# Modulation rows as VectorE dot products in the projection, the bonus ahead of the scaled keys, and query products in halves behind every group of gathered rows

## The chip, the cores and the metric

The kernel runs on one core of a Trainium2 chip, as one launch. The time is the device time of that core in microseconds, taken as the median of three runs. All data are 32-bit; "PE" is TensorE, "DVE" VectorE, "ACT" ScalarE, "POOL" GpSimd and "SP" SyncE, which here only issues DMAs. Line numbers (L...) are those of the kernel before.

## The reference, cut to what matters

One layer over 512 latent tokens and 256 context tokens of width 1024:

```
m = silu(c) @ w_mod + b_mod                       # 6 x 1024: shift, scale, gate, shift2, scale2, gate2
hx = rms_norm(x) * (1 + sc1) + sh1                # rows 1 and 2 (context: from c_ctx)
zx = hx @ w_in                                    # the projection, 3 x 1024 + lora columns + gates
k_dir = k * (1 + (iclr - 1) * k_a)                # per direction
bonus = sum(r * mean(k_dir) * r_k) * v            # per head of 64
... RWKV-7 scan in both directions, box pooling, sigmoid gates, output projection ...
x = x + gt1 * rms_norm(mix)                       # rows 3 of the modulation
hx2 = rms_norm(x) * (1 + sc2) + sh2               # rows 4 and 5
q = hx2 @ w_q; s = q . sub_keys                   # 8 heads x 2 halves, 128 keys each
top 16 of each half, top 16 of the 256 sums -> 16 experts per head and token
act = gelu(u_emb[idx] . hx2); out = sum(gate * act * v_emb[idx])
x = x + gt2 * rms_norm(out)                       # row 6
```

The last four of the six modulation rows (gt1, sh2, sc2, gt2; 4096 numbers, for `c` alone) are what the first part of the change computes in another way and at another place.

## The kernel before, in words

The stages follow each other with a barrier between: `front` (norm and the first two modulation rows), `project` (72 to 378 us), `gates` (to 530), `invert` (to 788), `scan`, `mix` (to 1292) and `peer` (to the end).

**`project`** works through 27 weight tiles (128 columns by 1024), 3 for the lora inputs and 3 for each of 8 head pairs j. Per tile SP loads the raw weights, ACT makes the high part (`high`, L446), DVE the low part (`low`, L553), PE multiplies 24 times per segment (`product`, lines 91 to 93), ACT copies with a scale (`scaled`, L451), DVE adds the shifted tokens (`shift`, L560 and L563). The order on every engine is written out by hand. DVE's iteration j does, for the tiles of pair j and for the vectors of pair j-1: shift, low, `unit`, `keys` (with the operand `tb` of the bonus), `queries`; `summed`, shift, low, `bounded`, `keys_out` (L620), `bonus` (L626); shift, low, `removal` (L635), `addition` (L642, L647). Three waits tie the others to it: ACT's first `scaled` of pair j waits for `addition` of pair j-2, its third `scaled` of pair j waits for `bonus(j-1)`, and PE's second `lora` of pair j waits for `bonus(j-1)`. The factor `kf` of the keys has two buffers. Results go to DRAM per field and pair, by SP, which waits for each in the order of its list.

**`invert`** inverts 32x32 blocks on DVE, in two halves b of 31 steps (L1136, L1138: a product and a sum per step); PE and ACT turn tiles before and after. Beside that PE makes the eight half rows of 512 of the last four modulation rows (`row`, L1226: one output partition, 8 products of 512 columns each), from 16 loads of 1 MB by SP; ACT copies each (L1094), PE turns it into a column (`column`, L1232), and DVE adds bias and gains (`columns`, L1120 to L1123). Two rows are made before the first half is turned out, six after it. `columns` stands in DVE's program between two steps of the second half:

```
if b and u == HB - 10:
    columns()        # first instruction: dve.wait_ge(s_col, NR)
```

**`peer`** has 32 steps s = 8 t + h (token tile t, head h), each of four groups q of four gathered rows (a gather brings 128 rows of 8 KB, u and v of one expert, 1.05 MB, issued by POOL at L2114 into a ring of 12 slots, of 16 from the second token tile on; a slot is free when PE has used it). Per group: four DVE dots (L2276), ACT gelu (L2186), DVE `gc_` (L2282), ACT four diagonal matrices (L2191), PE 8 products into the output (L2383, here V group). Queries and scores of all tokens are made in the first eight steps: three heads ahead of step 0, then in step s the head s+3: PE does `query(s+3, 0)` before V group 2, `query(s+3, 1)` before V group 3 (24 products each), and `score(s+3)` (L2362) behind V group 3. ACT, behind its work for group 3, copies query and scores (L2161, L2169 to L2175) and makes `exp(s+2)`, which needs two loads of its function table (L2037, L2186), and only then comes the gelu of the next step's group 0. DVE makes `best`, `pairs` and `numbers` of step s+2 behind groups 0, 1 and 2. In a step with queries SP also loads 2 x 0.52 MB of query weights and stores 0.39 MB of scores.

Of the kernel before, what the change touches and what calls it, by code (L numbers as in the profile page):

```python
# [95 lines left out]
def build(nc, x, ctx_in, gvec_in, wmod, wlora_in, wpair_in, pvec_in, lora_in, wz_in, wpool_in,  # L96
# [15 lines left out]
    with top:  # L112
# [15 lines left out]
        sc = sb(top, "sc", [P, KT, 2])  # L128
# [25 lines left out]
def front(nc, sb, sem, g):  # L154

    gv, mod, sc, ident, blk, bank, ht_hi, ht_lo = (g[k] for k in (
        "gv", "mod", "sc", "ident", "blk", "bank", "ht_hi", "ht_lo"))
    NB = 4
    with ExitStack() as st:
# [4 lines left out]
        modrow = sb(st, "modrow", [2, NB * 512])  # L164
        th = sb(st, "th", [P, 16])
# [131 lines left out]
def project(nc, sb, sem, g):  # L297
    gv, blk, bank, ht_hi, ht_lo, record = (g[k] for k in ("gv", "blk", "bank", "ht_hi", "ht_lo", "record"))
# [4 lines left out]
    with ExitStack() as st:  # L303
# [12 lines left out]
        kf = sb(st, "kf", [P, 2, NDIR, T])  # L316
# [8 lines left out]
        rec = sb(st, "rec", [P, RC_N])  # L325
        chunks = lambda a: a.rearrange("p (c s) -> p c s", s=CHUNK)
# [39 lines left out]
        with nc.Block() as block:  # L366
            @block.sync
            def _(sp):
# [18 lines left out]

                weights(0)
                weights(1)
                weights(2)  # L390
                sp.dma_start(pva[:, :, :], g["pvec_in"].rearrange("j p v -> p j v")).then_inc(s_pv, 16)
                lora_weights(0)
                lora_weights(1)
                for n in range(3, 8):
                    weights(n)
                for j in range(NPAIR + 1):
                    if j + 1 < NPAIR:
                        weights(3 * j + 8)
                    if j:
                        sp.wait_ge(s_r, 2 * j)  # L400
                        stored("r", j - 1)
                    if j < NPAIR:
                        sp.wait_ge(s_gc, j + 1)
                        stored("g", j)
                    if j + 2 < NPAIR:
                        weights(3 * j + 9)
                    if j:
# [5 lines left out]
                    if j + 2 < NPAIR:  # L413
                        weights(3 * j + 10)
                    if j:
# [9 lines left out]
                    if j + 2 < NPAIR:  # L425
                        lora_weights(j + 2)
                for f in FIELDS:
# [11 lines left out]
            def _(act):  # L439
# [50 lines left out]
                def rates(j):  # L490
# [5 lines left out]
                    for d in range(NDIR):  # L496
                        act.wait_ge(s_at, 4 * j + 2 * d + 2)
                        act.activation(kf[:, j % 2, d, :], al[:, j % 2, d, :], ACT.Identity, bias=col(j, OKA),
# [8 lines left out]
                high(1)  # L507
                act.wait_ge(s_vec, 1)
# [34 lines left out]
                exps(NPAIR - 1)  # L543

            @block.vector
            def _(dve):
# [46 lines left out]
                def keys(j):  # L593
                    k = zs[:, j % 2, 1, :]
                    for d in range(NDIR):
                        dve.wait_ge(s_kf, 2 * j + d + 1)
                        for C, view in parts(d):
                            o = chunks(kf[:, j % 2, d, :])[:, C, :]
# [4 lines left out]
                    ch(dve.tensor_tensor(tb[:, :], kf[:, j % 2, 0, CTX:T], kf[:, j % 2, 1, CTX:T][:, ::-1], ALU.add))  # L603
# [1849 lines left out]
```

## Time and profile before

| | |
|---|---|
| median of 3 runs (lowest, highest) | 2697.44 us (2691.69, 2699.06) |
| the profiled execution | 2706.24 us, its span 2704.5 us |
| granted TensorE clock, mean | 0.897 of full |
| busy share of the span | PE 81%, DVE 60%, ACT 32%, POOL 26% |
| moved by DMA | 741.53 MB, of it 536.90 MB by gathers |

The busy shares are means over stages with different limits, so a stage is read by itself: its busy time in a stretch (windows), the order of its instructions (timeline), and behind each instruction the time its engine sat idle and what ended that, in square brackets. PEclk 1.00 is the full clock of 2.4 GHz, 0.50 is 1.2 GHz. Start times are from the start of the span.

### The profile page before, as it was taken

To read this page: it belongs to the slowest core of one execution; us is meant where nothing else is said; L and a number is where in the kernel's file an instruction comes from. 1 tells how busy PE (TensorE), PEld (TensorE's weight loads), DVE (VectorE), ACT (ScalarE), POOL (GpSimd) and SP (SyncE) were. 2 spreads that over 40 slices of the span, in tenths; PEclk is the share of its full clock that TensorE was granted. 3 is DMA by queue.
4 is the path that set the end of the run, shared out by engine and by line. 5 is a ranking of instruction groups with operands and counts; after the bars stand their busy time and mean duration, and the time that the engine had idled before them with its cause. 6 is when DMAs were issued, how large, how long until landed. Compare 5 with 4: busy or idle time off the path is not lost.

```text
span 2704.5 us, 41392 instructions
## 1 busy us (share of the span) xinstructions
PE 2177.9 (81%) x16681; PEld 1362.7 (50%) x16681; DVE 1632.4 (60%) x3421; ACT 855.6 (32%) x1668; POOL 714.6 (26%) x607
## 2 busy tenths in 40 slices
PE   6899959887768989978789888777777777877777
PEld 2777748675258888857545443333232223333332
DVE  2489864358302434355486677777777777777764
ACT  4476733244143333422322222212212212222211
POOL 0000027000001111100233344544343444444441
PEclk8899979975858998979899999899998998888998
DMA  4245453252435242243699999999999999999995
GB/s 172 89 162 211 187 200 120 100 203 90 158 119 209 93 151 89 81 157 118 252 393 387 356 365 420 401 420 420 421 420 420 421 420 421 421 420 421 422 421 218
DMA packets 128832, 741.53 MB, mean 274 GB/s; under 512 B 17120, under 2 KB 24320, under 8 KB 60032
## 3 DMA queue, kind: packets, MB, share of 16 engines
q0 software_dynamic: 73728, 536.90, 48.2%
q1 hardware_dynamic: 53760, 199.89, 20.3%
q8 instruction: 131, 2.15, 0.3%
q10 hardware_dynamic: 1152, 2.10, 0.2%
q14 instruction: 61, 0.50, 0.1%
HBM read 683.14 MB, written 55.69 MB: 273 GB/s over the span
## 4 chain that ended last, share of the span: by engine, by line
DMA 28%; PE 15%; DVE 3%; issue 3%; ACT 2%; POOL 1%; POOLq 0%; DVEq 0%; ACTq 0%
DMA uv<-in_uv_in,ic 18%; PE bank L2383 12%; DMA uvx<-in_uv_in,ic 10%; DVE junk L2276 1%; PE bank L91 1%; PE bank L92 1%; PE bank L93 1%; POOL uv L2114 1%; DMA scores_dram<-later 1%; ACT dg L2191 0%; PE bank L2362 0%; ACT ge L2186 0%; ACT L2186 0%; DVE wql L2242 0%; POOL uvx L2114 0%
## 5 line engine op out<-in xcount | busy, mean ns | idle before, releaser
L2383 PE MATMUL bank<-uv,dg 128*128 128x512 f32 x1664 | 808.2, 642 | 230.7 <-ACT dg L2191 230.5
L2383 PEld LDWEIGHTS bank<-uv,dg 128*128 128x128 f32 x1664 | 333.4, 205 | 696.0 <-issue 395.5
L2276 DVE SCALAR_TENSOR_TENSOR junk<-uv,gr 128x1024 f32<-128x1024 f32 x416 | 509.8, 1225 | 218.1 <-DMA uv<-in_uv_in,ic 194.7
L2114 POOL DMA_INDIRECT uv<-in_uv_in,ic x416 | 462.5, 1112 | 648.7 <-PE bank L2383 583.1
L2186 ACT ACTIVATE ge<-dt_ 128x4 f32<-128x4 f32 x128 | 26.3, 205 | 928.7 <-DVE junk L2276 928.7
L2383 PE MATMUL bank<-uvx,dg 128*128 128x512 f32 x384 | 191.2, 656 | 62.6 <-ACT dg L2191 62.6
L2191 ACT ACTIVATE dg<-ident,gc_ 128x128 f32<-128x128 f32 x512 | 163.6, 390 | 29.4 <-DVE gc_ L2282 29.4
L91 PE MATMUL bank<-ht_hi,wh 128*128 128x256 f32 (+1 forms) x432 | 151.2, 350 | 22.9 <-DVE wl L553 22.9
L2383 PEld LDWEIGHTS bank<-uvx,dg 128*128 128x128 f32 x384 | 78.1, 209 | 175.6 <-issue 93.2
L2114 POOL DMA_INDIRECT uvx<-in_uv_in,ic x96 | 108.9, 1135 | 144.1 <-PE bank L2383 134.6
L92 PE MATMUL bank<-ht_lo,wh 128*128 128x256 f32 (+1 forms) x432 | 146.2, 338 | 0.0
L93 PE MATMUL bank<-ht_hi,wl 128*128 128x256 f32 (+1 forms) x432 | 145.8, 338 | 0.0
L2276 DVE SCALAR_TENSOR_TENSOR junk<-uvx,gr 128x1024 f32<-128x1024 f32 x96 | 117.5, 1224 | 41.8 <-DMA uvx<-in_uv_in,ic 37.7
L91 PEld LDWEIGHTS bank<-ht_hi,wh 128*128 128x128 f32 x432 | 82.8, 192 | 44.1 <-DVE wl L553 23.0
L818 POOL MEMSET uu<- 128x1920 f32 x4 | 6.6, 1703 | 308.1 <-POOLq L109 308.1
L92 PEld LDWEIGHTS bank<-ht_lo,wh 128*128 128x128 f32 x432 | 82.8, 192 | 9.4 <-issue 1.9
L93 PEld LDWEIGHTS bank<-ht_hi,wl 128*128 128x128 f32 x432 | 82.7, 191 | 8.7
L1368 POOL TENSOR_TENSOR lv<-lk,ec 128x1536 f32<-128x1536 f32 x8 | 22.1, 2761 | 238.4 <-PE bank L1601 238.4
L2282 DVE TENSOR_TENSOR gc_<-ge,pe_ 128x4 f32<-128x4 f32 x128 | 20.9, 163 | 97.8 <-ACT ge L2186 97.8
L91 PE MATMUL bank<-ht_hi,wzh 128*128 128x512 f32 x160 | 65.2, 408 | 17.9 <-DVE wzl L917 17.9
L1136 DVE TENSOR_TENSOR gm<-gz,gt 96x124 f32<-96x124 f32 (+15 forms) x62 | 55.2, 890 | 33.3 <-ACT gt L1060 31.1
L917 DVE TENSOR_TENSOR wzl<-wz,wzh 128x1024 fp32r<-128x1024 f32 x20 | 29.3, 1464 | 69.6 <-ACT wzh L866 69.6
(334 smaller groups left out, 3869.4 us busy)
## 6 DMA issues: line engine op xcount, KB each, us to landing
pair_record<-rec SPq DMA_DIRECT2D x40, 768.0 KB, 3.3
wm<-in_wmod SPq DMA_DIRECT2D x16, 1024.0 KB, 5.1
wraw<-in_wpair_in SPq DMA_DIRECT2D x24, 512.0 KB, 3.6
ab<-pair_record SPq DMA_DIRECT2D x16, 768.0 KB, 6.4
wz<-in_wz_in SPq DMA_DIRECT2D x20, 512.0 KB, 3.3
wm<-in_wmod SPq DMA_DIRECT2D x4, 2048.0 KB, 21.1
wraw<-in_wq_in SPq DMA_DIRECT2D x16, 512.0 KB
uv<-in_uv_in,ic POOLq DMA_INDIRECT x416, 27.6
```

The lines of the kernel that those rows point to most:

```text
L91: tensor.matmul(out, w_hi, x_hi, start=first, stop=False)
L92: tensor.matmul(out, w_hi, x_lo, start=False, stop=False)
L93: return tensor.matmul(out, w_lo, x_hi, start=False, stop=last)
L917: dve.tensor_tensor(wzl[:, n % 2, :, :], wz[:, n % 2, :, :], wzh[:, n % 2, :, :].bitcast(FP32), ALU.subtract).then_inc(s_lo, 1)
L1136: ch(dve.tensor_tensor(o, gz[:, :, 0:n, u:u + 1].broadcast_to((NU, 4, n, m)), gt[b][:, :, u:u + 1, n:HB].broadcast_to((NU, 4, n, m)), ALU. ...
L1368: pool.tensor_tensor(lv[:, :, :, :], lk[:, :, :, :], wide, ALU.mult).then_inc(s_kp, 1)
L2114: pool.indirect_dma_start(ring(i), None, g["uv_in"], bass.IndirectOffsetOnAxis(ap=ic[:, s % ICR, k:k + 1], axis=0)).then_inc(su[row_slot[i ...
L2186: act.activation(ge[:, GR * q:GR * q + GR], dt[:, GR * q:GR * q + GR], ACT.Gelu).then_inc(s_ge, 1)
L2191: act.activation(dg[:, n % 2, k, :], ident[:, :], ACT.Copy, scale=gc[:, n % 2, k:k + 1]).then_inc(s_dg, 1)
L2276: dve.scalar_tensor_tensor(junk[:, :], ring(i)[:, 0:D], 1.0, hc[:, t % 2, :], ALU.mult, ALU.mult, accum_out=dt[:, k:k + 1]).then_inc(s_ud, 1)
L2282: dve.tensor_tensor(gc[:, n % 2, :], ge[:, GR * q:GR * q + GR], rt.pe[:, s % ICR, GR * q:GR * q + GR], ALU.mult).then_inc(s_gc, 1)
L2383: mm = pe.matmul(acc(t, c)[:, :], dg[:, n % 2, k, :], ring(i)[:, D + 512 * c:D + 512 * c + 512], start=h == 0 and q == 0 and k == 0, stop= ...
```

## The change

1. The eight `row` products, their copies, `column` and `columns` leave `invert`, with their 16 loads. In `project` each of the 32 columns of 128 modulation values becomes one DVE dot product over 1024 elements, against silu(c) spread over all partitions; a transposed copy of the weights is loaded, 32 loads of 0.52 MB through three buffers. Four dots stand in each of DVE's iterations 0 to 7. `columns` stands in iteration 8 ahead of `removal`; PE turns the result and SP stores it at the stage's end.
2. In `project`, `bonus(j-1)` stands ahead of `keys_out(j-1)`, and `kf` has one buffer, for whose release ACT waits (`s_k`).
3. In `peer`, PE does half of a query product (12 products) behind every V group of steps 0 to 4, and the scores of head s+2 behind V group 0 of step s (1 to 5). ACT copies query 1 and scores and makes `exp(s+1)` behind its work for group 0, and copies query 0 behind group 2. DVE's `best`, `pairs`, `numbers` move one group later, `low` to groups 1 and 3.

```diff
@@ project, DVE @@
+                def dot(m):
+                    if m >= NM:
+                        return
+                    dve.wait_ge(s_wt[m % MR], 16 * (m // MR) + 16)
+                    if m:
+                        dve.wait_ge(s_dot, m)
+                    dve.scalar_tensor_tensor(cond[:, :], wt[:, m % MR, :], 0.5, silu[:, :], ALU.mult, ALU.mult,
+                                             accum_out=mc[:, m:m + 1]).then_inc(s_dot, 1)
...
                         low(3 * j + 5)
+                    dot(4 * j)
                     if j:
                         unit(j - 1)
                         keys(j - 1)
                         queries(j - 1)
+                    dot(4 * j + 1)
                     if j < NPAIR:
                         summed(j)
                         shift(3 * j + 4)
                         low(3 * j + 6)
                         bounded(j)
-                    if j:
+                    dot(4 * j + 2)
+                    if j:
+                        bonus(j - 1)
                         keys_out(j - 1)
-                        bonus(j - 1)
                     if j < NPAIR:
                         shift(3 * j + 5)
                         low(3 * j + 7)
+                    dot(4 * j + 3)
+                    if j == NPAIR:
+                        columns()
                     if j:
                         removal(j - 1)
                         addition(j - 1)
@@ project, SP @@
+                def row_weights(m):
+                    if m >= NM:
+                        return
+                    if m >= MR:
+                        sp.wait_ge(s_dot, m - MR + 1)
+                    sp.dma_start(wt[:, m % MR, :], g["wrow_in"][m]).then_inc(s_wt[m % MR], 16)
...
+                    row_weights(4 * j + 3)
                     if j:
                         sp.wait_ge(s_r, 2 * j)
                         stored("r", j - 1)
+                    row_weights(4 * j + 4)
@@ project, ACT, rates(j) @@
                         act.wait_ge(s_at, 4 * j + 2 * d + 2)
+                        if j:
+                            act.wait_ge(s_k, 2 * j)
@@ invert, DVE @@
-                        if b and u == HB - 10:
-                            columns()
@@ invert, PE @@
-                for n in range(EARLY):
-                    row(n)
                 turned_out(0)
                 combined(0)
-                pe.wait_ge(s_zc, 12)
-                column(0)
-                for n in range(EARLY, NR):
-                    row(n)
-                    column(n - 1)
-                column(NR - 1)
...
@@ peer, ACT @@
-                    if q >= 2 and s + 3 < HEADS:
-                        query(s + 3, q - 2)
+                    if q == 0 and 1 <= s and s + 2 < HEADS:
+                        query(s + 2, 1)
+                        score(s + 2)
+                    if q == 2 and s + 3 < HEADS:
+                        query(s + 3, 0)
...
-                if s + 3 < HEADS:
-                    score(s + 3)
-                if s + 2 < NS:
-                    exp(s + 2)
+                    if q == 0 and 1 <= s and s + 1 < NS:
+                        exp(s + 1)
@@ peer, DVE @@
-                    if q < 2 and s + 3 < HEADS:
-                        low(s + 3, q)
+                    if s == 0 and q == 0:
+                        low(3, 0)
+                    if q == 1 and s + 3 < HEADS:
+                        low(s + 3, 1)
+                    if q == 3 and s + 4 < HEADS:
+                        low(s + 4, 0)
...
-                    elif s + 2 < NS and q < 3:
-                        (best, pairs, numbers)[q](s + 2)
+                    elif s + 2 < NS and q > 0:
+                        (best, pairs, numbers)[q - 1](s + 2)
@@ peer, PE @@
                 for q in range(NQ):
-                    if q >= 2 and s + 3 < HEADS:
-                        query(s + 3, q - 2)
                     for k in range(GR):
...
-                if s + 3 < HEADS:
-                    score(s + 3)
+                    if q == 0 and 1 <= s and s + 2 < HEADS:
+                        score(s + 2)
+                    if s + 3 < HEADS:
+                        query(s + 3, q // 2, range(KT // 2 * (q % 2), KT // 2 * (q % 2) + KT // 2))
```

## Rows read from the trace of the kernel before

**Rows 1.** The profile's page, part 2: GB/s moved, in 40 slices of 67.6 us.

```profile
GB/s 172 89 162 211 187 200 120 100 203 90 158 119 209 93 151 89 81 157 118 252 393 387 356 365 420 401 420 420 421 420 420 421 420 421 421 420 421 422 421 218
```

**Rows 2.** Projection: busy us (x) of PE, PEld, DVE, ACT, POOL; PEclk, DMA share, GB/s.

```profile
172.00:327.00 155.00, 155.00 (x831) 122.76 (x829) 139.13 (x198) 111.43 (x164) 0.00 (x0) 1.00 0.53 198
```

**Rows 3.** Timeline of VectorE in the projection: start us, us, engine line op [idle before].

```profile
239.73 1.33 DVE L560 SCALAR_TENSOR_TENSOR zs<-bank,vva,zs 128x255 f32<-128x255 f32 x2 [1.02 <-ACT zs L451]
...
261.13 1.33 DVE L560 SCALAR_TENSOR_TENSOR rec<-bank,vva,rec 128x255 f32<-128x255 f32 x2 [1.83 <-ACT rec L451]
...
271.14 1.33 DVE L560 SCALAR_TENSOR_TENSOR zs<-bank,vva,zs 128x255 f32<-128x255 f32 x2 [1.02 <-ACT zs L451]
...
355.36 1.33 DVE L560 SCALAR_TENSOR_TENSOR rec<-bank,vva,rec 128x255 f32<-128x255 f32 x2 [2.97 <-ACT rec L451]
```

**Rows 4.** Timeline of VectorE in the router stage, one step.

```profile
1446.92 0.16 DVE L2282 TENSOR_TENSOR gc_<-ge,pe_ 128x4 f32<-128x4 f32 x1 [13.21 <-ACT ge L2186]
...
1453.15 0.08 DVE L2276 DVE_READ_ACCUMULATOR junk<-uv,gr 128x1 f32 x1
...
1457.52 0.16 DVE L2282 TENSOR_TENSOR gc_<-ge,pe_ 128x4 f32<-128x4 f32 x1 [0.27 <-ACT ge L2186]
...
1458.74 0.42 DVE L2012 TENSOR_TENSOR cand<-sv 128x256 f32<-128x256 f32 x1
...
1467.23 0.17 DVE L2282 TENSOR_TENSOR gc_<-ge,pe_ 128x4 f32<-128x4 f32 x1 [0.27 <-ACT ge L2186]
...
1470.95 1.22 DVE L2276 SCALAR_TENSOR_TENSOR junk<-uv,gr 128x1024 f32<-128x1024 f32 x1
...
1477.30 1.23 DVE L2276 SCALAR_TENSOR_TENSOR junk<-uv,gr 128x1024 f32<-128x1024 f32 x1
```

**Rows 5.** Timeline of VectorE in the inversion, around the column products.

```profile
683.04 1.02 DVE L1138 TENSOR_TENSOR gz<-gz,gm 96x828 f32<-96x828 f32 x1
725.65 0.77 DVE L1120 TENSOR_TENSOR colv<-bank,gv 128x8 f32<-128x8 f32 x4 [41.59 <-PE bank L1232]
...
727.17 0.95 DVE L1136 TENSOR_TENSOR gm<-gz,gt 96x768 f32<-96x768 f32 x1
```

**Rows 6.** Timeline of TensorE in the inversion, second half.

```profile
738.34 3.56 PE L1181 MATMUL bank<-ident,gz 96*128 96x96 f32 x20 [10.91 <-DVEq L1141]
```

**Rows 7.** Busy time of three stretches of the router stage, columns as in rows 2.

```profile
1345.00:1398.00 53.00, 44.77 (x128) 24.35 (x128) 41.49 (x112) 15.64 (x33) 18.37 (x16) 0.92 1.01 420
1398.00:1594.00 196.00, 172.77 (x512) 95.17 (x512) 130.19 (x312) 50.70 (x121) 69.83 (x64) 0.94 0.95 367
1594.00:1628.00 34.00, 29.81 (x59) 12.40 (x60) 30.16 (x76) 8.79 (x25) 15.97 (x14) 0.88 0.93 370
```

**Rows 8.** Timeline of TensorE in the router stage.

```profile
1441.26 1.95 PE L2362 MATMUL bank<-wor,qt_ 128*128 128x128 f32 x16
1447.57 8.83 PE L2383 MATMUL bank<-uv,dg 128*128 128x512 f32 x16 [4.36 <-ACT dg L2191]
...
1465.60 0.39 PE L93 MATMUL bank<-o_hi,wql 128*128 128x512 f32 x1
...
1470.51 0.40 PE L93 MATMUL bank<-o_hi,wql 128*128 128x512 f32 x1
...
1496.41 8.73 PE L2383 MATMUL bank<-uv,dg 128*128 128x512 f32 x16 [4.36 <-ACT dg L2191]
...
1647.66 7.13 PE L2383 MATMUL bank<-uv,dg 128*128 128x512 f32 x16 [3.00 <-ACT dg L2191]
...
1667.53 10.20 PE L2383 MATMUL bank<-uv,dg 128*128 128x512 f32 x16 [2.79 <-ACT dg L2191]
```

**Rows 9.** Timeline of ScalarE in the router stage.

```profile
1442.35 0.38 ACT L2169 ACTIVATE sc_<-bank 128x256 f32<-128x256 f32 x1 [6.22 <-PE bank L2362]
...
1443.86 1.28 ACT L2037 ACT_TABLE_LOAD   x1
...
1446.68 0.20 ACT L2186 ACTIVATE ge<-dt_ 128x4 f32<-128x4 f32 x1
```

More of the change, by code:

```diff
@@ L395, in _ @@
                     weights(n)
+                for m in range(MR):
+                    row_weights(m)
                 for j in range(NPAIR + 1):
@@ L507, in _ @@
                 high(1)
+                act.wait_ge(s_cb, 16)
+                act.activation(silu[:, :], cond[:, :], ACT.Tanh, scale=0.5).then_inc(s_cth, 1)
                 act.wait_ge(s_vec, 1)
@@ L543, in _ @@
                 exps(NPAIR - 1)
+                act.wait_ge(s_ct, 1)
+                act.activation(rw[:, :], bank[6][0:NM, 0:P], ACT.Copy).then_inc(s_rw, 1)
             @block.vector
@@ L1217, in combined @@
                         mm.then_inc(s_z, 1)
-                def row(n):
-                    for i in range(2):
-                        pe.wait_ge(s_wm[i], 16 * n + 16)
-                        if i == 0 and n >= 2:
-                            pe.wait_ge(s_rwc, n - 1)
-                        for k in range(KT // 2):
-                            c = KT // 2 * i + k
-                            mm = pe.matmul(bank[4 + n % 2][0:1, :], sc[:, c, 0:1], wm[:, i, k, :], start=c == 0, stop=c == KT - 1)
-                        mm.then_inc(s_rp, 1)
-                def column(n):
-                    pe.wait_ge(s_rwc, n + 1)
-                    for i in range(4):
-                        mm = pe.matmul(bank[6][:, 4 * n + i:4 * n + i + 1], rowv[:, n % 2, i * P:i * P + P], ident[0:1, 0:1],
-                                       start=True, stop=True)
-                    mm.then_inc(s_col, 1)
                 products(0)
@@ L2342, in _, with query @@
         def _(pe):
[L2343 to L2347 removed]
+            def query(h, b, ks=range(KT)):
+                if 0 in ks:
+                    pe.wait_ge(s_lo, 2 * h + b + 1)
+                    if h:
+                        pe.wait_ge(s_qc, 2 * h - 1 + b)
+                for k in ks:
                     mm = split_mm(pe, bank[2 + b][:, :], wh[:, b, k, :], wl[:, b, k, :], h2h[:, k, :], h2l[:, k, :],
                                   k == 0, k == KT - 1)
[L2350 removed]
+                if KT - 1 in ks:
+                    mm.then_inc(s_q, 1)
             def score(h):
```

112 lines of the change are left out of this document (44 added, 68 removed).

## The prediction

> **What bounds the kernel now.** I read the page's slices first, then busy time by stretch, then timelines. The slices show two kinds of kernel: until about 1285 us the DMA is far from its best, and from slice 21 to the last but one it moves 356 to 422 GB/s, mostly 420 [rows 1]. So the end is set by 512 gathers that stream at 420 GB/s, and an earlier stage is worth what it brings forward the start of that stream; within the stream only time counts in which the DMA is not full.
>
> The projection is bound by PE: in 155 us PE is busy for 155.00 at full clock, DVE for 139.13 [rows 2]. Its period is 271.14 - 239.73 = 31.41 us, and DVE idles in it twice, for 1.02 and 1.83 us [rows 3]. The inversion is bound by DVE, and there DVE stands still for 41.59 us: `columns` waits for the last column product while 8 steps of the second half are still to do [rows 5]. PE starts to turn that half out only when DVE is done, after 10.91 us idle [rows 6]. In the router stage step 0 runs at a full DMA (420 GB/s), steps 1 to 4 at 367 and step 5 at 370 [rows 7].
>
> **The inversion.** Without `columns` DVE goes on at 684.06 (683.04 + 1.02) instead of at 727.17 [rows 5]: 43.1 us. Late next could be PE, but its column work is gone too, and the wait in [rows 6] is for DVE alone; the store of the first half is issued when its copies end, before PE's column products began, so by DVE's order it is long past by then. The two rows made before the first half is turned out go as well; PE waited for DVE there, so nothing more is gained. I take -43.1, bounds -36 (if DMA or turning out shows up behind it) and -44.
>
> **The dots.** DVE gets 32 products of 1024 elements with a sum. The same form is in the trace: 1.23 us and 0.08 for the reading of the sum [rows 4], 1.31 each, 5.24 per period. DVE's period without its idle time is 31.41 - 2.85 = 28.56; with 5.24 of dots 33.8. That is over PE's 31.41, so DVE becomes the bound. Of the idle time I keep 0.5: DVE's first shift needs ACT's copy, which waits for `addition` just ahead of it, and the 1.02 in [rows 3] has both that copy and PE's lateness. The 1.83 goes, since `bonus` now stands ahead of `keys_out`: ACT may copy while DVE scales keys. The period is 34.3, +2.9. Pair 0 has room for its four dots (pair 1's vectors don't exist yet, DVE mostly waits); pairs 1 to 6 pay 6 x 2.9 = 17.6. In pair 7 the last two tiles have no low part and DVE idles 2.97 [rows 3], which takes most of three dots (3.9); the fourth is paid: 2.3. `columns` ahead of the last `removal` costs what it did, 727.17 - 725.65 = 1.5 [rows 5]; turning and storing its result lies beside 5.7 us of DVE work and the last stores. Sum +21.4.
>
> Moved past it: each row load on SP waits for a dot three back, which DVE has then passed; SP's list follows DVE's order, so neither stores nor weight loads fall behind. The DMA has room, at a share of 0.53 [rows 2]. ACT's new wait, with the last of its work of pair j queued behind it, is for `keys_out(j-1)`, which ends some 2 us after `bonus`; ACT first copies, makes a high part and tanh after `bonus`, so it costs nothing. If DVE gets later still, both get later together. Least: if dots overlap their neighbours and the sum is read for nothing, 1.1 each, +16. Most: PE. Its second `lora` waits for `bonus`, so that it now stands some 3 us per period (estimate from DVE's order). V groups behind idle times of 3.00 and 2.79 us took 7.13 and 10.20 us [rows 8]: the clock may stay or fall, at up to 3 us a time. PE's lead at that point is some 2 us, so at most 1 us per period shows, +29 with a little for waits. I take +21.4.
>
> **The clock.** The Trainium skill ("TensorE: Matmul & The Clock Gate", Why this matters for your kernels) says that an idle stretch between bursts puts the array back to half clock; by that rule each of seven gaps costs, and the projection would get some 28 us longer instead of 21. The trace bears it out in part: one of the two gaps above cost nothing. It is the base of two rivals.
>
> **The queries.** Four facts of a step of 48.84 us (1496.41 - 1447.57) [rows 8]: DVE stands 13.21 us before the first `gc_` [rows 4]; the scores stand behind V group 3 (1441.26) and ACT's copies and two table loads behind them (1442.35 to 1446.68 [rows 9]); PE idles 4.36 us and starts V group 0 at low clock, 8.83 us, where others take 7.13 [rows 8]. After the change I count from `gc_` of group 0. V group 0 starts at 0.65 (1447.57 - 1446.92) and ends at 7.8. PE makes the scores, ACT's copy can start 1.1 later, and from copy to gelu is 4.33 [rows 9]: 13.2, `gc_` at 13.4. Then `best` with one low part, dots, gelu: 10.6 (1457.52 - 1446.92), 24.0. Then `pairs` without a low part: 9.71 - 1.22 = 8.5, 32.5. Then low, `numbers` (3.72), gates (0.83) and dots (5.52): 11.3, 43.8 [rows 4]. PE needs four V groups of 7.13, scores of 1.95 [rows 8] and two queries of 24 products, 5.6 each (21 products start in the 4.91 us between two rows): 41.7. The DMA needs 16 x 1.05 + 1.05 + 0.39 = 18.2 MB, 43.3 us at 420. So 44 us per step, near a full DMA; 4.8 us gained, in step 4 6, since it has one low part less. In step 0 V group 2 no longer waits for a query, and step 1 starts some 6 us earlier, but the DMA is full there, so that is room, not time. Step 5 pays: it has scores but no queries, so by the same counts (no low parts) some 41 us for DVE, where the stretch before took about 34 [rows 7]. Its DMA needs 17.2 MB, 40.9 us at 420, so little shows.
>
> What counts is the DMA's empty time: 196 x (420 - 367)/420 = 24.7 us in steps 1 to 4, 34 x 50/420 = 4.0 in step 5 [rows 7], together 28.8, the most that can come. By my steps 0.7 us stays in each of three steps, 1.4 in step 4 and some tenths in step 5, about 4; I leave 6 for unevenness of a ring of 12, so -23, bounds -29 and 0. After step 8 `numbers` and gates meet behind group 3: 9.9 us of DVE against 10 of DMA per group, with 16 slots as cover; nothing.
>
> The Trainium skill ("ScalarE: Activation LUTs", What ACT_TABLE_LOAD costs) prices a change of table at about 2.66 us with a drain. By that `exp` would hold group 1 for 2.8 us longer, a step would take 46.6 and about 10 us of the gain would go. The row has 1.28, and the exponential's whole detour from 1443.86 to 1446.68 is 2.82 [rows 9]; I use the row.
>
> **Sum.** -43.1 + 21.4 - 23 = -44.7. The profiled execution took 2706.24 (span 2704.5); it would take 2661.5. That execution stands 8.8 above the median, 2697.44, which I carry over: 2652.7, say 2653. From no change, this measurement can tell about 0.3%, 8 us.
>
> **Rivals.** (A) *The query part is hidden or trades one wait for another.* The scores' wait moves from before group 0 to before group 1, 13.4 us against 10.6 for a group of that kind; if the ring of 12 empties there, only some 3 us come. 43.1 - 21.4 + 3 = 25: 2672. For it: DMA share is already 0.95 [rows 7]. Against: the rate in GB/s is not. 0.2.
> (B) *DVE in the projection costs more than its length*, by PE's clock or by ACT's `kf` wait: +29 to +32. 43 - 31 + 21 = 33: 2664. 0.14.
> (C) *Slower.* The gap ahead of the second `lora` takes PE to 1.2 GHz and keeps it there: a period, all of it PE [rows 2, 3], would take up to twice 31.41, less the part in which the gap has not yet told, some 53 us in all. 7 x 21.6 = +151, against it 43 and 23: 2782. It decides where low clock fills over half of each period, +74 in the stage. Against: after 4.36 us idle V group 0 took 8.83 and the next ran full, so PE recovers within a group [rows 8]. 0.04.
> (D) *The inversion doesn't do what it says*: the 41.59 us turn into a wait for something that the trace hides behind it; +21 - 23: about 2697. For it nothing but that the wait hides it. 0.05.
> (E) The forecast, 0.57.
>
> **Range and chances.** The forecast's own bounds: -44 + 16 - 29 = -57, and -36 + 29 - 10 = -17; with a few us of spread of the median, 2637 to 2680. That takes in A and B and leaves out C, D and the outer ends, 0.15 to 0.2. A, B and E are faster by over 0.3%: with D's better half 0.9. Same 0.05, slower 0.05.
>
> **What would show it.** Right: `columns` in the projection, no wait of 41 us in the inversion, whose second half ends 43 us sooner after its start; dots of 1.31 us; a projection period near 34.3 with DVE never idle beyond 0.5 us, PE idle some 3 us ahead of the second `lora`; steps 1 to 4 at 44 us with 410 GB/s or more, the wait before group 1 at 7 us on DVE. Wrong: a period beyond 35.5 (clock or waits), dots that wait for their rows (SP's order), steps still at 47 or more, or a new wait in the inversion on PE or a store.

## The result, and the profile after

The changed kernel takes 2652.56 us (median of 4 runs, 2647.50 to 2666.96); the kernel before took 2696.35 in the same comparison. The ratio is 0.984, interval 0.9813 to 0.9867: 36 to 50 us shorter. Forecast: 2653, 44.7 shorter. The profiled execution has a span of 2653.7 us against 2704.5.

By stage, from the start times of the same instruction in both traces (us; a step is measured from `gc_` to `gc_`):

| stage | before | after | change | forecast |
|---|---|---|---|---|
| front, to the first shift | 115.0 | 112.9 | -2.1 | 0 |
| projection, to the first instruction of gates | 266.9 | 283.1 | +16.2 | +21.4 |
| gates | 188.5 | 189.2 | +0.7 | 0 |
| inversion, first step to the scan's first DVE sum | 228.7 | 186.0 | -42.7 | -43.1 |
| scan and mix, to the first `gc_` | 545.6 | 545.3 | -0.3 | 0 |
| router, steps 0 to 7 | 364.6 | 340.2 | -24.4 | -23 |
| router, the rest | 995.2 | 997.0 | +1.8 | 0 |

**Slices.** The same line of the page as [rows 1]:

```profile
GB/s 175 146 205 251 245 200 162 83 215 1 49 180 158 111 134 137 36 177 110 267 420 417 408 393 415 415 420 420 421 420 420 421 420 420 420 420 421 421 420 209
```

Where the line of before dips to 356 and 365 in slices 23 and 24, this one dips to 408 and 393.

**Projection.** DVE in one period of the kernel after (timeline, columns as in [rows 3]):

```profile
244.11 1.33 DVE L594 SCALAR_TENSOR_TENSOR zs<-bank,vva,zs 128x255 f32<-128x255 f32 x2 [0.65 <-ACT zs L479]
...
247.54 1.22 DVE L690 SCALAR_TENSOR_TENSOR cond<-wt,silu 128x1024 f32<-128x1024 f32 x1
248.68 0.08 DVE L690 DVE_READ_ACCUMULATOR cond<-wt,silu 128x1 f32 x1
248.68 1.01 DVE L625 SCALAR_TENSOR_TENSOR uk<-zs,vva,rn 128x768 f32<-128x768 f32 x1
...
267.03 1.28 DVE L594 SCALAR_TENSOR_TENSOR rec<-bank,vva,rec 128x255 f32<-128x255 f32 x2
...
277.64 1.33 DVE L594 SCALAR_TENSOR_TENSOR zs<-bank,vva,zs 128x255 f32<-128x255 f32 x2 [0.54 <-ACT zs L479]
```

The period is 277.64 - 244.11 = 33.53, forecast 34.3. Both idle times of [rows 3] answer here: 1.02 became 0.54, 1.83 is gone. A dot costs 1.14, from 247.54 to the start of the next instruction, not 1.31: the sum's reading starts at 248.68, and so does `unit`. Four times 0.17 is 0.7 of the 0.8 us by which the period is shorter than forecast. From 176 to 345 us the only thing that DVE waits for is ACT's first copy: it never waits for a row load, nor ACT for the release of `kf`.

PE now waits ahead of the second `lora` (timeline of TensorE):

```profile
231.80 2.94 PE L770 MATMUL bank<-lin,lw 64*128 64x256 f32 x8 [2.06 <-DVE rec L660]
265.44 1.57 PE L770 MATMUL bank<-lin,lw 64*128 64x256 f32 x8 [0.55 <-DVE rec L660]
298.98 1.92 PE L770 MATMUL bank<-lin,lw 64*128 64x256 f32 x8 [2.06 <-DVE rec L660]
```

It waits 0.5 to 2.1 us, where 3 were estimated, and the eight products took 2.94 once and 1.92 once instead of 1.57: a dip of the clock. Behind the last of these rows it reaches into the next weight tile, whose first twelve products take 0.35 to 0.58 us (mostly 0.41) instead of 0.28, up to 303.5. The period from 210.47 to 244.11 has a granted clock of 0.95, the next one 1.00, and yet they differ by only 0.1 us (33.64 and 33.53): DVE is the bound by then, so the dips cost next to nothing.

**Inversion.** The step in front of which `columns` stood (DVE), the turning out of the second half (TensorE), and the first sum of the scan (DVE):

```profile
664.69 1.02 DVE L1155 TENSOR_TENSOR gz<-gz,gm 96x828 f32<-96x828 f32 x1
...
710.16 3.58 PE L1196 MATMUL bank<-ident,gz 96*128 96x96 f32 x20 [29.28 <-DVEq L1156]
...
771.21 0.69 DVE L1446 TENSOR_TENSOR ka<-bank,mgt 128x512 f32<-128x512 f32 x1 [58.73 <-PE bank L1550]
```

The wait of 41.59 is gone and no other took its place; PE waits for DVE, as in [rows 6], and longer, since it has nothing else to do.

**Router.** The windows that answer to [rows 7] (the last column is GB/s), then the four `gc_` of a step:

```profile
1364.00:1538.00 174.00, 164.48 (x504) 90.08 (x505) 127.89 (x306) 50.19 (x118) 74.27 (x63) 0.99 1.01 413
1538.00:1581.00 43.00, 33.72 (x90) 15.93 (x88) 30.75 (x79) 10.94 (x29) 18.59 (x17) 0.96 0.96 382
```

```profile
1452.63 0.16 DVE L2266 TENSOR_TENSOR gc_<-ge,pe_ 128x4 f32<-128x4 f32 x1 [0.27 <-ACT ge L2169]
...
1465.92 0.16 DVE L2266 TENSOR_TENSOR gc_<-ge,pe_ 128x4 f32<-128x4 f32 x1 [7.96 <-ACT ge L2169]
...
1476.51 0.16 DVE L2266 TENSOR_TENSOR gc_<-ge,pe_ 128x4 f32<-128x4 f32 x1 [0.27 <-ACT ge L2169]
...
1485.07 0.17 DVE L2266 TENSOR_TENSOR gc_<-ge,pe_ 128x4 f32<-128x4 f32 x1 [0.27 <-ACT ge L2169]
```

Groups of 13.3, 10.6 and 8.6 us, and 11.0 from there to the next step; forecast 13.4, 10.6, 8.5, 11.3. DVE's wait ahead of group 1 is 7.96, forecast 7. The eight steps take 47.5, 45.2, 43.5, 43.5, 42.4, 42.1, 34.9 and 41.1, where before they took 53.4, 48.9, 48.8, 48.8, 48.9, 33.9, 39.5 and 42.4. In steps 1 to 4 the rate is 413 instead of 367 GB/s, and TensorE's granted clock 0.99 instead of 0.94. That last number was in no step of the forecast.

### The profile page after: what moved, and what is told of

Read it like the earlier page. It is cut to its first block, busy times and chain, and to the rows that moved or that the text cites. A ratio compares the mean times of both kernels' runs of the same rounds, so it can differ in the third digit from the quotient of the medians.

```text
span 2653.7 us, 41107 instructions
## 1 busy us (share of the span) xinstructions
PE 2117.1 (80%) x16489; PEld 1345.7 (51%) x16489; DVE 1670.8 (63%) x3486; ACT 849.1 (32%) x1661; POOL 737.5 (28%) x607
## 3 DMA queue, kind: packets, MB, share of 16 engines
q0 software_dynamic: 73728, 536.90, 48.8%
## 4 chain that ended last, share of the span: by engine, by line
DMA 30%; PE 13%; DVE 4%; issue 3%; ACT 2%; POOL 1%; POOLq 0%; DVEq 0%; ACTq 0%
DMA uvx<-in_uv_in,ic 27%; PE bank L2371 10%; DVE junk L2260 2%; DMA uv<-in_uv_in,ic 1%; POOL uvx L2097 1%; DMA scores_dram<-later 1%; PE bank L91 1%; PE bank L93 1%; PE bank L92 1%; ACT dg L2174 0%; PE bank L2352 0%; DVE wql L2226 0%; ACT ge L2169 0%; ACT L2169 0%; POOL uv L2097 0%
## 5 line engine op out<-in xcount | busy, mean ns | idle before, releaser
L2097 POOL DMA_INDIRECT uv<-in_uv_in,ic x416 | 481.7, 1158 | 624.3 <-PE bank L2371 550.5
L2097 POOL DMA_INDIRECT uvx<-in_uv_in,ic x96 | 112.6, 1173 | 124.0 <-PE bank L2371 114.2
L91 PEld LDWEIGHTS bank<-ht_hi,wh 128*128 128x128 f32 x432 | 83.7, 194 | 45.2 <-DVE wl L587 23.0
L1153 DVE TENSOR_TENSOR gm<-gz,gt 96x124 f32<-96x124 f32 (+15 forms) x62 | 55.2, 891 | 33.7 <-ACT gt L1100 31.6
```

What stands on the lines that cost most here:

```text
L91: tensor.matmul(out, w_hi, x_hi, start=first, stop=False)
L1153: ch(dve.tensor_tensor(o, gz[:, :, 0:n, u:u + 1].broadcast_to((NU, 4, n, m)), gt[b][:, :, u:u + 1, n:HB].broadcast_to((NU, 4, n, m)), ALU. ...
L2097: pool.indirect_dma_start(ring(i), None, g["uv_in"], bass.IndirectOffsetOnAxis(ap=ic[:, s % ICR, k:k + 1], axis=0)).then_inc(su[row_slot[i ...
```

## The experiments

Executions of one kernel lie up to 32 us apart. The largest part of that which the profiles show is in scan and mix: the same instructions took 545 us at a granted clock of 0.90 in the profiles before and after, and 527 at 0.94 in another (below). So an edit is judged by its own stage in the profiles, and the medians stand beside it. Over all profiles with the same instructions in a stage, the projection repeats within 0.1 us, steps 0 to 7 of the router within 1.6, the inversion within 2.1 and the gates stage within 4 (185.6 to 189.4).

### Each part alone

The kernel before with the router stage of the kernel after:

> The kernel before with the third part alone (query halves, scores behind V group 0). Theory (the parts add up, and the router part is worth what it takes out of the time in which the DMA is not full): steps 1 to 4 at 43.5 us instead of 48.9, step 5 at 42, the projection period at 31.41 and the 41.6 us wait in the inversion as before; 23 us shorter than before, about 2673 us. Rival (the router part only pays because the stage starts at another moment, or the parts hide each other): gain under 12 us or over 35 us.

The kernel after with the router stage of the kernel before:

> The changed kernel with the router stage of before, so parts 1 and 2 alone. Theory: projection about 14 to 16 us longer, inversion 43 us shorter, router stage 53.4 and 48.9 us per step as before: 27 us shorter than before, about 2669 us. Rival (time won ahead of the stream of gathers is partly lost inside it): the router stage gets longer than before and less than 20 us remain.

| | projection | inversion steps | router, steps 0 to 7 | median | ratio to before |
|---|---|---|---|---|---|
| before | 266.9 | 167.4 | 364.6 | 2698.97 | |
| router part alone | 266.9 | 169.0 | 339.9 | 2673.63 | 0.9906 (0.9877 to 0.9934) |
| parts 1 and 2 alone | 283.1 | 124.4 | 364.6 | 2667.86 | 0.9882 (0.9851 to 0.9912) |
| all | 283.1 | 124.4 | 340.2 | 2652.56 | 0.984 (0.9813 to 0.9867) |

The last row's ratio is from the comparison in which before had 2696.35. By stages the parts add up: each stage has the same length with and without the other part, and time won ahead of the gathers arrives at the end (the rest of the router takes 995 to 997 us in all four). The spans of the profiles, too, fall by 27.3 and 23.9 us for the parts and by 50.8 for all. The medians don't show it: 25 and 31 us by parts are 56, where all together gives 44 (36 to 50). Nothing in the stages answers to these 12 us; they are of the size of the spread between executions.

### What the dots cost

```diff
-                    dve.scalar_tensor_tensor(cond[:, :], wt[:, m % MR, :], 0.5, silu[:, :], ALU.mult, ALU.mult,
+                    dve.scalar_tensor_tensor(cond[:, 0:64], wt[:, m % MR, 0:64], 0.5, silu[:, 0:64], ALU.mult, ALU.mult,
```

> The changed kernel with every dot over 64 of its 1024 elements (the other 960 are left out, so the four modulation rows are wrong sums; loads, waits and order stay). Theory (the dots' length on DVE is the whole price, PE is the bound without it): the period falls from 33.54 back to 31.4 to 31.6 us, the projection is 13 to 16 us shorter than in the changed kernel, the rest alike: about 2638 us. Rival (the price is in waits: loads on SP, kf, the bonus wait of PE): the period stays above 32.5 us.

Projection 268.9 us, 14.2 shorter; period 31.41; median 2631.73, ratio 0.9769 (0.9729 to 0.9809). DVE idles in both old places again:

```profile
229.41 1.33 DVE L594 SCALAR_TENSOR_TENSOR rec<-bank,vva,rec 128x255 f32<-128x255 f32 x2 [1.38 <-ACT rec L479]
239.41 1.33 DVE L594 SCALAR_TENSOR_TENSOR zs<-bank,vva,zs 128x255 f32<-128x255 f32 x2 [0.88 <-ACT zs L479]
```

So 14 of the 16 us are the length of the dots: 12.8 in the six full periods and 1.3 in pair 7. Pair 0 costs nothing, as forecast (30.45 us from its first shift to that of pair 1, before, after and here). With short dots DVE has 2.3 us of slack per period, in which a small price of the waits could hide; but in the kernel after, where it has none, the period is no longer than 28.56 + 4 x 1.14 + 0.54 = 33.66. So loads, semaphores and the release of `kf` cost nothing that shows. The other 2.0 us lie behind the last full period, where `columns` and its turning stand: from the first shift of pair 7 to the gates stage it is 50.0 us here and 48.0 before.

### The bonus ahead of the scaled keys

```diff
-                        bonus(j - 1)
                         keys_out(j - 1)
+                        bonus(j - 1)
```

> The changed kernel with part 2 undone: keys_out ahead of bonus, kf still single. Theory (part 2 is what takes the second idle time of a period away): bonus ends 1.8 us later, ACT's third copy waits for it by 0.6 us or more and DVE for ACT; the period goes from 33.54 to between 34.2 and 35.4 us, PE waits up to 4 us ahead of its second lora, 5 to 13 us longer than the changed kernel, projection stage. Rival (DVE is bound by its own work, ACT stands behind its logarithm and exponential anyway): the period stays 33.5 to 33.7 us and the time stays.

Period 34.14 us, projection 286.8, 3.7 longer than after. That is between the two expectations and nearer to the rival's. The median, 2648.87 (ratio 0.9847, 0.9793 to 0.9902), doesn't tell it from the kernel after. DVE's timeline:

```profile
235.54 1.33 DVE L594 SCALAR_TENSOR_TENSOR rec<-bank,vva,rec 128x255 f32<-128x255 f32 x2 [0.46 <-ACT rec L479]
246.21 1.33 DVE L594 SCALAR_TENSOR_TENSOR zs<-bank,vva,zs 128x255 f32<-128x255 f32 x2 [0.54 <-ACT zs L479]
```

Without part 2 only 0.46 of the 1.83 us comes back. The forecast credited part 2 with all of the 1.83; most of it goes because a dot fills it. Part 2 is worth 0.6 us a period.

### The inversion: order or work?

In the kernel before, `columns` moved behind the last step and the copy of the second half, with PE's row products left as they were:

```diff
-                        if b and u == HB - 10:
-                            columns()
                     dve.sem_inc(s_inv, 1)
                     dve.tensor_copy(gy[b], gz[:, :, :, :].rearrange("u k s t -> u s k t")).then_inc(s_gy, 1)
+                    if b:
+                        columns()
```

> The kernel before with one edit: the addition of the column products stands behind the last step of the second half of the inversion and behind its copy, instead of 8 steps before the end; PE's row products stay. Theory (the 41.6 us are PE's row products, DVE's place in the order adds only what could run beside them): DVE's remaining 8 steps and copy, 12 us, run beside PE, so PE starts to turn the half out 8 to 11 us sooner; 8 to 11 us shorter than before, where taking the products off PE gives 43. Rival (the wait is a matter of order alone): 30 us or more shorter.

```profile
692.73 2.29 DVE L1140 COPY gt<-gz 96x4096 f32<-96x4096 f32 x1
722.42 0.77 DVE L1120 TENSOR_TENSOR colv<-bank,gv 128x8 f32<-128x8 f32 x4 [27.40 <-PE bank L1232]
...
785.39 0.69 DVE L1463 TENSOR_TENSOR ka<-bank,mgt 128x512 f32<-128x512 f32 x1 [61.60 <-PE bank L1567]
```

DVE is done at 695 and waits 27.40 us; from its first step, at 567.77, to the scan's first sum it is 217.6 us, 11.0 less than before and 31.6 more than after. Median 2690.39, ratio 0.9957 (0.9933 to 0.9981). So 11 of the 43 us were a matter of DVE's order, to be had by moving one call, and 32 come from PE's row products, which stand in front of the turning out on PE.

That doesn't show that the products have to leave PE. In the kernel after, PE stands idle for 30.45 and 29.28 us ahead of the two turnings out. A row with its column takes some 8.8 us here (its loads included), so an estimate from these rows is that six of the eight fit into that idle time. Whether another order on PE alone would have brought most of the 32 us, without the dots' 16 us in the projection, was not tried; it is the rival that this case leaves open.

### Which edit of the router part pays?

First, edits of the kernel after. Query products whole, at the same end points:

```diff
-                    if s + 3 < HEADS:
-                        query(s + 3, q // 2, range(KT // 2 * (q % 2), KT // 2 * (q % 2) + KT // 2))
+                    if s + 3 < HEADS and q % 2:
+                        query(s + 3, q // 2)
```

> The changed kernel with the query products whole again, at the same two end points: nothing behind V groups 0 and 2, 24 products behind V groups 1 and 3; scores stay behind V group 0. Theory (the gain comes from the scores' place; halves only spread 5.6 us of PE work evenly): steps 2 to 4 at 43.5 to 45 us, at most 5 us longer in all. Rival (the halves carry the gain, since a V group behind a whole query frees its slots 2.8 us late): steps at 46.5 us or more, 12 us or more longer.

Scores back behind V group 3 of the step before (on ACT the same move):

```diff
@@ PE @@
-                    if q == 0 and 1 <= s and s + 2 < HEADS:
-                        score(s + 2)
...
+                if s + 3 < HEADS:
+                    score(s + 3)
```

> The changed kernel with the scores behind V group 3 again (halves kept, exponential kept behind group 0's work, scores of head s+3 in step s). Theory (the scores' place is what costs: V group 3, half a query, two copies, scores and three copies stand in one chain ahead of the gelu of group 0): about 2.8 to 3.5 us more per step than the changed kernel, steps 1 to 4 at 46.3 to 47.5 us, 10 to 14 us longer in all. Rival (halves and the even spread are the gain): steps stay at 43.5 to 44.5 us.

Both theories fell. Whole queries: steps 2 to 4 at 46.6, 46.9 and 46.5 us, steps 0 to 7 13.5 us longer (median 2662.82, ratio 0.9861, 0.9823 to 0.9899). Scores last: steps 1 to 4 at 43.1 and steps 0 to 7 at 338.3, 1.9 shorter than after (2649.85; 0.982, 0.9771 to 0.9868). The place of the scores, on which the forecast's argument was built, is worth nothing. The edit left the exponential behind group 0, so of the copies, scores and exponential that the forecast moved as one piece, this clears only the first two.

Then edits of the kernel before: halves alone, the exponential behind the activations of group 0 alone, and both. The first is the first block, the second the second:

```diff
@@ PE @@
                 for q in range(NQ):
-                    if q >= 2 and s + 3 < HEADS:
-                        query(s + 3, q - 2)
...
                         mm.then_inc(s_vd, 1)
+                    if s + 3 < HEADS:
+                        query(s + 3, q // 2, range(KT // 2 * (q % 2), KT // 2 * (q % 2) + KT // 2))
@@ ACT @@
+                    if q == 0 and 1 <= s and s + 1 < NS:
+                        exp(s + 1)
                 if s + 3 < HEADS:
                     score(s + 3)
-                if s + 2 < NS:
-                    exp(s + 2)
```

> The kernel before with the query products in halves behind every V group and nothing else: scores, copies and the exponential's detour stay behind group 3. Theory (one chain ahead of a step's first gelu sets the step as long as it is over the DMA's 43.3 us: last V group, what PE has to do ahead of the scores, copies, scores, copies, exponential): half a query instead of a whole one stands in it, 1.8 to 2.8 us less per step, steps 1 to 4 at 46 to 47 us, router stage 7 to 11 us shorter. Rival (the halves by themselves bring the DMA's rate): steps at 44.5 us or less. Rival 2 (no gain alone): 48.5 us.

> The kernel before with the exponential one step later, behind the activations of group 0, and nothing else: queries whole, scores behind V group 3. Theory (the same chain): the 2.8 us from the end of the scores' copies to the gelu leave it; steps 1 to 4 at 45.7 to 46.5 us, router stage 9 to 12 us shorter. Rival (the exponential is hidden, or delays group 1 by as much): steps at 48 us or more.

> Both of the last two edits in the kernel before: halves, and the exponential behind group 0. Theory (they add up in one chain until the DMA's 43.3 us bind): steps 1 to 4 at 43.3 to 44.5 us, step 5 at 34 to 36 us, router stage 20 to 26 us shorter than before, with the scores and DVE's three parts at their old places. Rival (DVE's parts one group later, or the scores behind group 0, are needed): steps at 46 us or more.

| | step 0 | steps 1 to 4, mean | steps 5 to 7 | steps 0 to 7 | median | ratio to before |
|---|---|---|---|---|---|---|
| before | 53.4 | 48.9 | 115.8 | 364.6 | 2698.22 | |
| halves alone | 50.6 | 47.8 | 113.3 | 355.3 | 2685.22 | 0.9966 (0.9944 to 0.9988) |
| exponential alone | 50.5 | 47.6 | 112.6 | 353.5 | 2686.66 | 0.996 (0.9943 to 0.9977) |
| both | 47.6 | 44.0 | 113.2 | 337.1 | 2669.55 | 0.99 (0.9879 to 0.992) |
| scores last | 47.6 | 43.1 | 118.4 | 338.3 | | |
| after | 47.5 | 43.6 | 118.2 | 340.2 | | |

In steps 1 to 4 each edit alone gives 1.0 to 1.3 us, less than either expectation had, and both give 4.8: there they don't add up as lengths in one chain would. In step 0 they do (2.9, 3.0 and 5.8 us); the totals of 9.3 and 11.1 us lie in the expected ranges only by that. Both together give 27.5, a little over the expected 20 to 26. The timeline of TensorE says why steps 1 to 4 behave so. Halves alone:

```profile
1472.05 9.33 PE L2383 MATMUL bank<-uv,dg 128*128 128x512 f32 x16 [4.36 <-ACT dg L2191]
1484.03 7.03 PE L2383 MATMUL bank<-uv,dg 128*128 128x512 f32 x16
```

The exponential alone:

```profile
1483.43 7.13 PE L2383 MATMUL bank<-uv,dg 128*128 128x512 f32 x16 [1.41 <-ACT dg L2191]
1494.03 8.83 PE L2383 MATMUL bank<-uv,dg 128*128 128x512 f32 x16 [3.46 <-ACT dg L2191]
```

Both:

```profile
1466.36 7.13 PE L2383 MATMUL bank<-uv,dg 128*128 128x512 f32 x16 [1.41 <-ACT dg L2191]
1476.96 7.13 PE L2383 MATMUL bank<-uv,dg 128*128 128x512 f32 x16 [0.67 <-ACT dg L2191]
1486.73 7.07 PE L2383 MATMUL bank<-uv,dg 128*128 128x512 f32 x16
```

The kernel after:

```profile
1466.57 7.13 PE L2371 MATMUL bank<-uv,dg 128*128 128x512 f32 x16 [1.55 <-ACT dg L2174]
1477.16 7.13 PE L2371 MATMUL bank<-uv,dg 128*128 128x512 f32 x16 [0.66 <-ACT dg L2174]
```

Whole queries in the kernel after:

```profile
1451.73 9.77 PE L2371 MATMUL bank<-uv,dg 128*128 128x512 f32 x16 [4.36 <-ACT dg L2174]
```

Of steps 2 to 4, each that takes over 46 us, in any version, has one gap of PE of 3.46 or 4.36 us, and each that takes less has none over 1.6. (In step 1 a gap can go unpunished: whole queries in the kernel after take 43.8 us there with one of 4.36.) With halves alone the exponential still holds PE for 4.36 us ahead of V group 0. With the exponential moved alone that gap falls to 1.41, but without half a query behind V group 0 another of 3.46 opens ahead of V group 1. Each time the V group behind the long gap runs in part at 1.2 GHz (granted clock 0.81 over the 8.83 us of the last row of the exponential alone, 1.00 over the 7.13 us of the row before it) and takes 8.8 to 9.9 us instead of 7.1. So an edit alone saves part of a gap and keeps the other gap and the slow group; both together drop all of it. Windows over steps 1 to 4, with PE's busy time first and its granted clock third from the end:

Halves alone, the exponential alone, both, and the scores last:

```profile
1376.00:1567.00 191.00, 171.19 (x512) 94.43 (x512) 129.76 (x308) 50.09 (x117) 73.49 (x64) 0.96 0.97 388
```

```profile
1388.00:1578.00 190.00, 170.87 (x512) 94.35 (x512) 129.28 (x308) 49.70 (x118) 68.42 (x64) 0.96 0.97 379
```

```profile
1378.00:1554.00 176.00, 165.20 (x512) 91.27 (x512) 129.02 (x309) 49.24 (x118) 72.91 (x64) 1.00 1.01 420
```

```profile
1360.00:1532.00 172.00, 163.89 (x512) 91.86 (x512) 128.64 (x307) 49.64 (x119) 75.31 (x64) 1.00 1.01 421
```

Before, PE was busy for 172.77 of 196 us [rows 7]: 23 idle, and 8 to 9 busy beyond the 164 that the same products take at full clock. Those are the 4 x 1.7 of the slow V groups, and a little of what runs behind them. With both edits it is 11 idle and 165 busy, and the stream of gathers is full, at 420 GB/s. The steps of "both" are 1 us longer than those of "scores last", from which only DVE's order in the router sets it apart, but its steps 5 to 7 are 5.2 us shorter; in all it is 1.2 us ahead.

The Trainium skill ("TensorE: Matmul & The Clock Gate", Why this matters for your kernels) warns of idle gaps between bursts of matmuls, since they put the array back to half clock. The trace agrees: gaps of 3.46 and 4.36 us did that, gaps of 1.41 and 1.55 in these steps didn't. Between them the length of the gap alone doesn't decide: [rows 8] has 3.00 without and 2.79 with it, and step 0 of the kernel after has it behind 1.84:

```profile
1330.66 8.83 PE L2371 MATMUL bank<-uv,dg 128*128 128x512 f32 x16 [1.84 <-ACT dg L2174]
```

### The dots where DVE has room

Here the dots stand only where DVE has room. Four stand in pair 0, one in each of pairs 1 to 6, two in pair 7, and twenty in the gates stage, two behind the low part of each of its first ten tiles; their rows land in the space of `wb`, which is loaded after them. `columns` stands at the end of that stage.

```diff
@@ gates, DVE @@
                     dve.tensor_tensor(wzl[:, n % 2, :, :], wz[:, n % 2, :, :], wzh[:, n % 2, :, :].bitcast(FP32),
                                       ALU.subtract).then_inc(s_lo, 1)
+                    for e in (2 * n, 2 * n + 1):
+                        if K0 + e < NM:
+                            dot(e)
@@ gates, SP @@
-                    if n == NW:
+                    if n == 12:
+                        sp.wait_ge(s_dot, NM - K0)
                         sp.dma_start(wb[:, :, :, :], g["wb_in"]).then_inc(s_wb, 16)
```

> The changed kernel with its 32 dots spread otherwise: four in pair 0 of the projection, one in each of pairs 1 to 6, two in pair 7, and twenty in the gates stage, two behind the low part of each of its first ten tiles, where DVE stands about 4 us per tile; the columns are made at the end of that stage. Theory (dots cost only where DVE has no slack): projection period back to PE's 31.4 us, projection 12 to 15 us shorter than in the changed kernel, gates stage within 2 us of its length; about 2640 us. Rival (the dots disturb GpSimd's pooling or the weight loads in the gates stage): that stage grows by 8 us or more and the gain is gone.

Median 2636.48, ratio 0.9786 (0.9728 to 0.9843). Projection 271.1, 12.0 shorter than after; its period is 31.74, not 31.41. Gates 193.8, 4.6 longer than after, and 4.4 longer than in any profile without dots in that stage: between the two expectations. Two timelines of the gates stage, VectorE and GpSimd:

```profile
402.77 1.33 DVE L1006 TENSOR_TENSOR wzl<-wz,wzh 128x1024 fp32r<-128x1024 f32 x1 [3.29 <-ACT wzh L934]
404.02 2.31 DVE L990 SCALAR_TENSOR_TENSOR gy<-wb,silu 128x1024 f32<-128x1024 f32 x1
...
406.45 2.13 DVE L990 SCALAR_TENSOR_TENSOR gy<-wb,silu 128x1024 f32<-128x1024 f32 x1
...
409.65 1.21 DVE L990 SCALAR_TENSOR_TENSOR gy<-wb,silu 128x1024 f32<-128x1024 f32 x1
```

```profile
403.10 2.15 POOL L921 TENSOR_TENSOR pl<-cb,icn 128x512 f32<-128x512 f32 x1
405.33 2.17 POOL L922 TENSOR_TENSOR pl<-pl,uu 128x512 f32<-128x512 f32 x1
407.56 1.71 POOL L926 MEMSET ca<- 128x1920 f32 x1
409.32 1.71 POOL L926 MEMSET cb<- 128x1920 f32 x1
```

A dot takes 1.22 us beside GpSimd's memset and 2.1 to 2.3 beside its two-input products. The Trainium skill ("SBUF — State Buffer", SBUF: two separate sides) calls the pair of SBUF ports that GpSimd shares with VectorE an exclusive lock, held for a whole instruction; VectorE with two SBUF inputs meets it only against a GpSimd instruction that reads SBUF. These rows agree: the memset, which reads nothing, disturbs no dot, and the others end in turn, each some 1.1 to 1.2 us behind the end of the other engine's (405.25, 406.33, 407.50, 408.58).

With this placing of the dots and the router stage of "scores last":

> The dots of the kernel with twenty of them in the gates stage, and the router stage with halves, the exponential behind group 0 and the scores behind V group 3 in the step before. Theory: projection 271 us and gates 194 us as there, steps 0 to 7 together 338 us in place of 341; about 12 us below the changed kernel, 2633 to 2641 us. Rival (the starts that shift bring other gaps in the stream): within 4 us of the changed kernel.

Median of 5 runs 2638.29, ratio 0.9783 (0.9761 to 0.9805). That interval lies wholly below the one of the kernel after (0.9813 to 0.9867, from its own comparison with before). Projection 271.1, gates 193.7, steps 0 to 7 337.9: by stages 9.8 us less than after, 7.5 of it by the dots' place and 2.3 in the router. These two versions can't be told apart by their medians, and the first one's interval (0.9728 to 0.9843) overlaps that of the kernel after.

## Why the prediction was right, step by step

**The total** was right, 2653 against 2652.56. By the two profiles the gain is 50.8 us, 6.1 more than forecast: 5.2 from the dots, 1.4 from the router, 2.1 from a front that happened to be shorter, less 2.6 in small terms. The medians give 43.8; the difference between the two is well inside what scan and mix vary by. So the exact hit is luck. The range was met by terms of the right size, one of them, the router's, with a cause that the runs don't bear out.

**The inversion** (-43.1, measured -42.7): right, with the reason given. The moved `columns` shows what the forecast did not separate: 11 us are its place in DVE's order, 32 PE's row products where they stand on PE.

**The dots** (+21.4, measured +16.2): the mechanism was right, DVE becomes the bound and keeps 0.54 us of idle time where 0.5 was forecast. The term that was off is 1.31 us a dot. It added the reading of the sum to the product, but the next instruction starts with that reading unless it waits for the dot, and here it doesn't: 1.14. Over six periods that makes 4.1 of the 4.8 us by which pairs 1 to 6 came out lower (12.8 for 17.6, itself 0.2 more than the 6 x 2.9 it stands for). The lower bound had named this case, at 1.1 each and +16; it was the right end. In the router the dots do start 1.34 us apart, but there each waits for the one before.

**Part 2** was credited with DVE's 1.83 us per period. With the old order only 0.46 comes back, and the period grows by 0.60. Its worth is 3.7 us in all.

**The new waits.** ACT's wait for `kf` and SP's row loads cost nothing, as forecast; with short dots the period is 31.41 again. PE's gap ahead of the second `lora` was 0.5 to 2.1 us, not 3, and the clock dipped behind it for a few microseconds at most, inside DVE's longer period, so rivals B and C didn't come true. (B's sum takes 21 for the queries where the forecast has 23, and the range takes 10 as their least where the text had said 0; neither changes the forecast.)

**The queries** (-23, measured -24.4): the size was right and the four groups came out within 0.3 us, but the cause was not the one given. The forecast laid the gain to moving the scores, with the copies and the exponential, from before group 0 to before group 1. With the scores back it stays whole; with the scores, and DVE's three parts, at their old places and two edits alone it is 27.5 us. Of the piece that the forecast moved, only the exponential counts, and only together with the halves. The bound that it drew from the DMA's empty time, 28.8 us as the most that can come, stood. What pays is that half a query and a free ACT keep PE's gaps short: less idle time, and in steps 2 to 4 no V group at 1.2 GHz. The forecast had this row, 4.36 us and 8.83 [rows 8], and did not draw the rival from it in the right place; it feared the clock in the projection, where it cost nothing, and did not count what the clock would give back in the router, 8 us of PE's busy time in four steps. Moving the scores even costs 2.1 us, in step 1 (45.2 against 43.1 with the scores last); steps 2 to 4 take 43.1 us either way. Step 5 takes 42.1 us in place of 33.9 (forecast 41), but that is not the scores' doing: with the scores last steps 5 and 6 together take 77.0 us, and 77.1 in the kernel after. Before they took 73.4, of which step 7 gives 1.3 back, so "so little shows" was a little too kind, by 2.4 us.

**Rival A** (one wait for another, 13.4 us ahead of group 1 empties the ring) fell: that group took 13.3 us and the DMA stayed at 413 GB/s.

**Still open.** Whether another order of the row products on PE would have served as well as the dots. Why the clock in scan and mix is 0.90 in one execution and 0.94 in another with the same instructions. And what else, beside its length, makes a gap cost clock.

## What to carry to other kernels

Work taken off the bound engine is worth what its stage's wait shows, and it is cheapest where the receiving engine idles, not where its period is nearly full: 20 dots moved from one stage to another gave 7.5 us. Two edits that shorten a wait of TensorE can each look nearly worthless alone if either leaves one gap long enough to cost its clock; test them together before dropping one. When a forecast is right in size, undo its named cause once: here the cause was another.

## What the runs showed of the hardware that was not expected

- A dot with a sum costs 1.14 us to the next instruction, not 1.31; two that wait for each other cost 1.34.
- The V group behind a gap of 3.46 or 4.36 us takes 8.8 to 9.9 us instead of 7.1; behind 1.41 or 1.55 it doesn't, but behind 1.84 and 2.79 it did, and behind 3.00 it didn't.
- Scan and mix run 18 us shorter in some executions of the same instructions. Windows of the kernel after, and of the one with the keys first:

```profile
771.00:1316.00 545.00, 470.11 (x9310) 414.89 (x9304) 226.97 (x469) 182.41 (x323) 79.78 (x37) 0.90 0.39 139
```

```profile
774.00:1301.00 527.00, 452.87 (x9307) 399.86 (x9303) 226.56 (x469) 182.75 (x324) 80.33 (x37) 0.94 0.40 143
```

  PE's busy time differs by 17 us with its clock, all else is alike. That hides an effect of 4 us in any median of a few runs.
- A DVE product of two inputs in SBUF takes 2.1 to 2.3 us instead of 1.22 in the rows shown while GpSimd works on two inputs.
